# Expert rounds that serve one group of 32 slots each, with the activations turned on VectorE

## The reference

```python
logits = (x @ w_router) + b_router
top_v, top_e = lax.top_k(logits, 4)
gates = softmax(top_v)
# for each expert e, on the tokens that chose it:
gu = xe @ w_gu[e] + b_gu[e]                       # 1024 -> 2048
gate = minimum(gu[:, :1024], 7.0)
up = clip(gu[:, 1024:], -7.0, 7.0)
act = (up + 1.0) * gate * sigmoid(1.702 * gate)
y[token] += (act @ w_down[e] + b_down[e]) * gate_of(token, e)
```

## Time and profile before

| | us |
|---|---|
| median of three runs | 1610.37 |
| lowest and highest | 1606.5, 1611.21 |
| span of the profiled execution | 1606.3 |
| PE busy in it | 1577.0 (98%) |
| DVE, ACT, POOL busy | 791.2, 272.1, 209.5 |
| DMA over the span | 505.80 MB, mean 315 GB/s |

### The profile page before, as it was taken

How to read it: one execution, slowest core, us unless ns; L and a number is a source line. 1 busy time by engine, 2 the same in 40 slices (tenths; PEclk the granted TensorE clock), 3 DMA queues, 4 the chain that set the end, 5 groups by cost and what they waited for, 6 DMA issues and landing times.

```text
span 1606.3 us, 33098 instructions
## 1 busy us (share of the span) xinstructions
PE 1577.0 (98%) x13439; PEld 731.2 (46%) x13439; DVE 791.2 (49%) x1687; ACT 272.1 (17%) x554; POOL 209.5 (13%) x269
## 2 busy tenths in 40 slices
PE   9999999999999899999999999999999999999996
PEld 7677487787846333333333333333333333333332
DVE  4359639506424654445444554445444554445445
ACT  2310120006212111111111111111111111111113
POOL 3624300015100001000100001000100001000100
PEclk9999999999998899999999999999999999999998
DMA  7455746622362799999999999999999999999982
GB/s 242 153 176 191 242 165 202 234 63 112 131 257 102 262 381 404 404 402 400 404 395 405 406 404 391 405 404 403 400 393 410 402 397 395 404 404 402 400 341 106
DMA packets 72716, 505.80 MB, mean 315 GB/s; under 512 B 14577, under 2 KB 15025, under 8 KB 47434
## 3 DMA queue, kind: packets, MB, share of 16 engines
q1 hardware_dynamic: 60338, 485.32, 76.1%
q0 software_dynamic: 12320, 19.73, 4.8%
HBM read 495.93 MB, written 26.04 MB: 325 GB/s over the span
## 4 chain that ended last, share of the span: by engine, by line
PE 95%; DVE 1%; ACT 1%; issue 1%; POOL 1%; DMA 0%; SPq 0%; DVEq 0%; POOLq 0%; ACTq 0%
PE PS L1283 42%; PE PS L897 16%; PE PS L1290 14%; PE PS L1296 7%; PE PS L1206 3%; PE PS L948 2%; PE PS L1013 2%; PE PS L1327 1%; PE PS L1316 1%; PE PS L999 1%; PE PS L1063 1%; PE PS L962 1%; POOL weight_ring L604 1%; PE PS L1108 0%; PE PS L1192 0%
## 5 line engine op out<-in xcount | busy, mean ns | idle before, releaser
L1283 PE MATMUL PS<-weight_ring,region_experts 128*32 128x512 f32 x5376 | 679.4, 594 | 0.8 <-ACT region_experts L819 0.8
L1283 PEld LDWEIGHTS PS<-weight_ring,region_experts 128*32 128x32 f32 x5376 | 188.5, 110 | 345.7 <-issue 339.8
L1290 PE MATMUL PS<-weight_ring,act_turned 128*32 128x512 f32 x2048 | 231.4, 592 | 0.0
L1283 PE MATMUL PS<-ring_more,region_experts 128*32 128x512 f32 x768 | 228.2, 593 | 0.0
L897 PE MATMUL PS<-region_x,region_w 128*128 128x260 f32 (+1 forms) x928 | 209.4, 385 | 1.0 <-DVE region_x L1501 1.0
L897 PEld LDWEIGHTS PS<-region_x,region_w 128*128 128x128 f32 x928 | 175.2, 190 | 33.1 <-issue 4.6
L1681 DVE STREAM_TRANSPOSE region_experts<-region_x 32x256 f32<-32x256 f32 x384 | 166.8, 434 | 4.9
L656 POOL DMA_INDIRECT y_acc<-region_x,idx_y x31 | 49.2, 1586 | 783.0 <-ACT region_x L850 706.1
L1290 PEld LDWEIGHTS PS<-weight_ring,act_turned 128*32 128x32 f32 x2048 | 66.6, 110 | 139.5 <-issue 134.0
L1296 PE MATMUL PS<-weight_ring,act_turned 128*32 128x256 f32 x2048 | 128.9, 380 | 0.0
L1698 DVE TENSOR_TENSOR region_experts<-PS,region_w 128x512 f32<-128x512 f32 x32 | 22.1, 691 | 192.8 <-PE PS L1283 192.8
(11 more groups left out here) (290 smaller groups left out, 1288.8 us busy)
## 6 DMA issues: line engine op xcount, KB each, us to landing
weight_ring<-w_gu SPq DMA_DIRECT2D x112, 2048.0 KB, 10.3
weight_ring<-w_down SPq DMA_DIRECT2D x64, 2048.0 KB, 10.1
ring_more<-w_gu SPq DMA_DIRECT2D x16, 2048.0 KB, 13.6
region_w<-w_mt SPq DMA_DIRECT2D x33, 512.0 KB, 4.2
weight_ring<-cache_kT SPq DMA_DIRECT2D x64, 256.0 KB, 4.0
weight_ring<-cache_v SPq DMA_DIRECT2D x64, 256.0 KB, 3.9
weight_ring<-w_out SPq DMA_DIRECT2D x2, 2048.0 KB, 10.2
weight_ring<-bias_strip SPq DMA_DIRECT2D x1, 2560.0 KB, 12.2
```

Source lines behind the costliest of these rows:

```text
L1283: mm = pe.matmul(out[GRP * j:GRP * j + GRP], hTe[u][:, k, GRP * g:GRP * g + GRP], weights(c, u)[:, k, :], start=(k == 0), stop=(k == KD - 1))
L1290: pe.matmul(bank(3)[GRP * j:GRP * j + GRP], actT[:, k, GRP * g:GRP * g + GRP], w_dn[:, k, 512 * q:512 * q + 512], start=(k == 0), stop=(k ...
```

## The change

- A gate/up chunk is now two of the eight contraction blocks k, with all 2048 columns, ordered in four quarters of 256 gate and the 256 up columns that belong to them. A round serves one group g: its four matmuls side by side take the same 32 stationary columns and the four quarters of one k (`gu_step`). All four chunks are read in each round; chunk 0 has two places, and slots are freed in the third round (`gu_free`).
- With that, one partition block of a bank holds gate and up of the same columns of one group, and DVE's `group` does the whole activation of a group behind its round.
- One DVE transpose of 128x256 a group (32x32 blocks) writes `actT`. The rows of `w_down` are ordered to match. The eight PE transposes and the three ACT copies are gone.
- The gate of a slot is applied by ACT in the copies to `ysc`, six of them instead of four; `spread_gates` sums the gate parts by six small reductions, behind a new wait of DVE for `y_ready`.
- `down_wide` has groups 0 and 1, `down_rest` group 2; `down_wide` runs over all k before `down_rest`.
- 96 slots instead of 128 in `compare`, `pick`, gather and scatter; the bias has 512 columns instead of 1536.
- The down chunks lie in slots 0 and 1, gate/up in 2 to 5; so gate/up of expert 0 is loaded early and down late.

```diff
-            def ring_load(c, e):
-                if c < 4:
-                    src = w_gu[bass.ds(e, 1), c].rearrange("a p x -> (a p) x")
...
+            def gu_load(c, e, u=0):
+
+                src = w_gu[bass.ds(e, 1), c].rearrange("a p x -> (a p) x")
+                more = c == 0 and u
+                sp.dma_start(W7[:, :] if more else W6[:, slot(2 + c):slot(3 + c)], src).then_inc(r_full[6 if more else 2 + c], 16)
+
+            def down_load(c, e):
+                src = w_down[bass.ds(e, 1), c].rearrange("a p x -> (a p) x")
                 sp.dma_start(W6[:, slot(c):slot(c + 1)], src).then_inc(r_full[c], 16)
...
-            def load(b, e, u, second=True):
+            def load(b, e, u, whole=True):
                 n = b * NE + e
-                sp.wait_ge(S["round_done"], (n - 1) * ROUNDS + 1)
-                ring_load(0, e)
+                if whole:
+                    gu_load(0, e, u)
                 sp.wait_ge(S["b_wide_done"], n)
                 bias_load(e)
-                if second:
-                    second_load(e, u)
-                sp.wait_ge(S["round_done"], (n - 1) * ROUNDS + 2)
-                ring_load(2, e)
+                for c in range(1, 3):
+                    sp.wait_ge(S["gu_free"], (n - 1) * 3 + c + 1)
+                    gu_load(c, e)
                 sp.wait_ge(S["round_done"], (n - 1) * ROUNDS + 3)
-                ring_load(3, e)
+                gu_load(3, e)
                 for c in range(2):
                     sp.wait_ge(S["down_done"], (n - 1) * 2 + c + 1)
-                    ring_load(4 + c, e)
+                    down_load(c, e)
...
+                    for h in range(2):
+                        act.activation(ysc[u][0:64, 512 * h:512 * h + 512], bank(3)[64 * h:64 * h + 64], ACT.Copy,
+                                       scale=gate_a[u][64 * h:64 * h + 64])
                     act.wait_ge(S["down_done"], ne * 2 + 2)
...
+                    for j in range(4):
+                        ins = act.activation(ysc[u][64:CAP, QW * j:QW * j + QW], bank(4, QW)[GRP * j:GRP * j + GRP], ACT.Copy,
+                                             scale=gate_b[u][GRP * j:GRP * j + GRP])
+                    ins.then_inc(S["y_ready"], 1)
...
+            def gu_step(g, u, k):
+
+                for q in range(4):
+                    mm = pe.matmul(bank(g)[GRP * q:GRP * q + GRP], hTe[u][:, k, GRP * g:GRP * g + GRP],
+                                   weights(k // 2, u)[:, k % 2, SEG * q:SEG * q + SEG], start=(k == 0), stop=(k == KD - 1))
+                return mm
...
-                    pe.wait_ge(r_full[0], (ne + 1) * 16)
-                    pe.wait_ge(r_full[6 if u else 1], (b * (NE // 2) + i + 1) * 16)
                     pe.wait_ge(S["hTe_ready"], b * SELS + e + 1)
-                    gu_round(bank(0), u, ((0, 0), (0, 1), (0, 2), (1, 2)))
+                    for k in range(KD):
+                        if k == 0:
+                            pe.wait_ge(r_full[6 if u else 2], (b * (NE // 2) + i + 1) * 16)
+                        elif k % 2 == 0:
+                            pe.wait_ge(r_full[2 + k // 2], (ne + 1) * 16)
+                        mm = gu_step(0, u, k)
+                    mm.then_inc(S["round_done"], 1)
                     pick(b * SELS + e + 2, e + 1, 1 - u)
...
+                    for k in range(KD):
+                        mm = gu_step(2, u, k)
+                        if k in (1, 3, 5):
+                            mm.then_inc(S["gu_free"], 1)
+                    mm.then_inc(S["round_done"], 1)
+
+                    pe.wait_ge(S["actT_ready"], ne * ROUNDS + 2)
                     pe.wait_ge(S["y_ready"], ne + 1)
...
+                    for kk in range(KD):
+                        if kk % 4 == 0:
+                            pe.wait_ge(r_full[kk // 4], (ne + 1) * 16)
+                        mm = down_wide(kk)
+                    mm.then_inc(S["wide_done"], 1)
+                    pe.wait_ge(S["actT_ready"], ne * ROUNDS + 3)
+                    for kk in range(KD):
+                        mm = down_rest(kk)
+                        if kk % 4 == 3:
+                            mm.then_inc(S["down_done"], 1)
...
+            def group(ne, g):
+
+                gu, sg, a = gu_t[g % 2], sg_t[g % 2], act_t[g % 2]
+                n = ne * ROUNDS + g + 1
+                dve.wait_ge(S["round_done"], n)
+                dve.tensor_tensor(gu, bank(g), b_wide, ALU.add).then_inc(S["biased"], 1)
...
+                dve.transpose(actT[:, :, GRP * g:GRP * g + GRP], a.rearrange("p (k x) -> p k x", k=KD)).then_inc(S["actT_ready"], 1)
...
-                    index(b * SELS + e + 2, 1 - u, floats=last and u == 0)
...
+                    group(ne, 0)
+                    slot_rows(b * SELS + e + 2, 1 - u, taken=ne + 1, floats=last and u == 0)
+                    group(ne, 1)
+                    group(ne, 2)
```

More of the change, by code:

```diff
@@ L268, in build_step @@
         sum4 = small(201, 5)
-        gcol = [small(206 + n) for n in range(2)]
-        spare = small(208)
-        unused = [small(209 + n) for n in range(2)]
+        gate_a = [small(206 + n) for n in range(2)]
+        gate_b = [small(208 + n) for n in range(2)]
+        spare = small(210)
+        unused = [small(211 + n) for n in range(2)]
         top_v = part(WR, 3936, NTILE, 8)
@@ L493, in experts @@
                         load(b, i * 2 + u, u)
-            second_load(1, 1)
-            load(0, 1, 1, second=False)
+            gu_load(0, 1, 1)
+            load(0, 1, 1, whole=False)
             experts(0, 1)
@@ L1272, in weights @@
             def weights(c, u):
-                if c == 1 and u:
-                    return W7[:, :].rearrange("p (k x) -> p k x", k=KD)
-                return W6[:, slot(c):slot(c + 1)].rearrange("p (k x) -> p k x", k=KD)
-            w_dn = W6[:, slot(4):slot(6)].rearrange("p (k x) -> p k x", k=KD)
-            def gu_round(out, u, units, ks=range(KD)):
-                for k in ks:
-                    for j, (c, g) in enumerate(units):
-                        mm = pe.matmul(out[GRP * j:GRP * j + GRP], hTe[u][:, k, GRP * g:GRP * g + GRP], weights(c, u)[:, k, :], start=(k == 0), stop=(k == KD - 1))
-                if k == KD - 1:
-                    mm.then_inc(S["round_done"], 1)
@@ L1298, in down_rest @@
+            def down_rest(kk):
+                for j in range(4):
+                    mm = pe.matmul(bank(4, QW)[GRP * j:GRP * j + GRP], actT[:, kk, 64:CAP], w_dn[:, kk, QW * j:QW * j + QW],
+                                   start=(kk == 0), stop=(kk == KD - 1))
                 return mm
@@ L1614, in _, with spread_gates @@
             L(dve.tensor_scalar(posv[:, :, 0:NE], rt_eg[:, :, 0, :], -1.0, None, ALU.add))
+            def spread_gates(src, u):
+                for h in range(2):
+                    dve.tensor_reduce(gate_a[u][64 * h:64 * h + 64], src[0:64], AX.X, ALU.add)
+                for j in range(4):
+                    ins = dve.tensor_reduce(gate_b[u][GRP * j:GRP * j + GRP], src[64:CAP], AX.X, ALU.add)
+                ins.then_inc(S["gates_set"], 1)
             def gates():
@@ L1671, in slot_rows @@
                 dve.tensor_tensor(idx_i[u][0:CAP, :], sl[0:CAP, 0:1], unused[u][0:CAP], ALU.subtract).then_inc(S["idx_ready"], 1)
+                if taken is not None:
+                    dve.wait_ge(S["y_ready"], taken)
+                    spread_gates(sl[:, 3:6], u)
             def keep(u):
@@ L1740, in pair @@
                     dve.sem_inc(S["may"], 1)
-                    turn_rows(1 - u)
+                    if not (last and u == 1):
+                        turn_rows(1 - u)
                     if last and u == 0:
```

215 lines of the change are left out of this document (78 added, 137 removed).

## The result

The changed kernel takes 1596.1 us (median of four runs, 1593.89 to 1597.41) beside 1609.88 us for the kernel before on the same chip: a ratio of 0.9917, interval 0.9903 to 0.9932. It is faster by 13.8 us where 34.6 were forecast; the time lies in the range, near its upper end. Its profiled execution spans 1595.5 us.

What follows compares the result with a forecast made beforehand. PE was taken to pace the kernel, with DMA 1.2 us an expert behind. Savings of 28.6 us (28 experts), 5.7 (four others) and 0.3 (end) made 34.6; span 1571.7 plus 4.1 gave 1576 us, range 1563 to 1602.

Steps and rivals of the forecast that it cites:

- What bounds the kernel before: Expert stage: PE, without gaps, paces the loads at 32.72 us an expert; DMA needs 31.5, only 1.2 less.
- PE's own need: PE's work in one expert once the transposes are gone: 31.25 to 31.3 us.
- The price of the transposes on PE: Two sets of four 128x128 transposes an expert: 1.42 us x 32 experts, 45.4 us, all on the path.
- The transpose on DVE: Each new 128x256 transpose, three an expert, taken at 0.434 us, at most 1.74; hidden.
- DVE's margin of 1.8 us: Gathered rows turned on DVE at 29.5 us of an expert, wanted by PE at 31.3; 0.5 at dear transposes.
- rival (c): DVE or the gather becomes late, rows turned 1 us after PE wants them: 32.3 an expert, 1597 us; chance 0.07.
- The mechanism: Gate/up chunks, freed late and wanted early, let DMA pace the stage after two or three experts; small first-round PE waits.
- the need of DMA: Per expert, 29.3 us for six weight loads plus 2.2 for indirect gather and scatter: 31.5 us.
- the wait at chunk 3: Gate/up chunk 3 lands at 35.7, wanted at 36.4: margin 0.7 us, then 0.2 us an expert above DMA's 31.5.
- (a): DMA's lower rate late in an expert is contention, not waiting: 32.1 to 32.7 an expert, 1589 to 1608 us; chance 0.22.
- (b): PE waits 2 us at chunk 3 each first round and its clock may drop: 1629 to 1680 us; chance 0.13.
- (d): DMA has more to give, PE alone paces the experts: 45.7 us won, 1564.6 us; chance 0.10.

Runs made afterwards that it cites:

- run 1: Kernel before without its eight PE transposes an expert, ScalarE copying the activations unturned, old load schedule kept: 1572.4 us, ratio 0.9776.
- e4_noboth: Kernel after with gather and scatter bounded to row 0, so nearly no token rows move: 1562.9 us (one run).
- e12_bal128_inter: Kernel after with the kernel before's slot order, gather and scatter over 128 slots, groups 0 and 1 in one double round, earlier slot_rows: 1571.5 us.
- Runs 8, 10, 11 and 13 to 15: Kernel after, old slot order, 128 slots 1589.2 us; gather only 128 1589.5; run 1 at 96 1628.8; e12_bal128_inter with gather 96 1612.1, scatter 96 1585.7, gather 112 1615.3.
- e9_ord128: Kernel after with gather and scatter over 128 slots again, its own slot order kept: 1600.1 us.
- e8_bal128: Kernel after with the kernel before's slot order and gather and scatter over 128 slots: 1589.2 us.
- run 2: Kernel after with groups 0 and 1 served chunk by chunk in one double round, slot_rows earlier, PE awaiting the routing's count before the stage: 1594.9 us, ratio 0.9919.
- Run 3: Kernel after with gate/up chunk 3 of later experts loaded for only 64 of 128 partitions: 1642.0 us (one run).

## Why the prediction was wrong

**Right.** What bounds the kernel before (PE, with DMA 1.2 us an expert behind it): run 1 removes PE's work alone and gets 36 us. PE's own need, 31.25 to 31.3: 31.38 in e4_noboth and e12_bal128_inter. The price of the transposes on PE, 45.4 us: PE's busy time falls from 1577.0 to 1531.3 in e4_noboth, 45.7. The transpose on DVE at 0.434: it took 0.45. DVE's margin of 1.8 us: the rows are turned at 1046.27 + 5.36 = 1051.63, and the next expert begins behind the down product at about 1053.4; rival (c) did not happen. The mechanism, that the period becomes that of the loads, through a wait on gate/up in the first round: the chain shows just that, with chunk 3 as the one that ends last.

**Wrong: the need of DMA, 31.5 us an expert.** The sum was 29.3 for the weights and 2.2 for the indirect transfers, taken from the earlier trace rows of the kernel before as if the change left them alone. It did not. The diff takes both transfers from 128 slots to 96; I counted that line as fewer compare columns and a smaller pick, and put no price, not even bounds, on the gather and the scatter themselves. No term of the sum stood for that edit. What the runs showed in its place is 32.33 us an expert in the kernel after, against 31.38 without the rows (e4_noboth, 33 us less in all). Runs 8, 10, 11 and 13 to 15 show the price of 96 slots in the order of the kernel before: 15 us in the new schedule, 56 in the old one, 48 in the double round. In the order of the kernel after, 96 slots alone cost nothing against 128 (e9_ord128, 1600.1), so there the number, the order and the schedule have to change together. The rest of the DMA sum was sound: with 128 slots, the old order and the double round (e12_bal128_inter) the engines deliver 13.1 MB in 31.38 us and PE waits for chunks 1.1 us in all, and in e1_noturn an expert bound by its loads takes 31.55 to 31.90.

**Wrong: the size of the wait at chunk 3.** The forecast gave 0.7 us of margin, used up after two or three experts, and 0.2 us of stall on top of DMA's need; so its middle lay 11.4 us above PE alone (1576.0 to 1564.6). With 128 slots in the old order (e8_bal128, 1589.2) the kernel lies 26.3 us above PE alone (e4_noboth, 1562.9): 18.8 us are waits for gate/up, 0.6 an expert, and 5.4 us are a longer busy time of PE (1536.7 for 1531.3), which comes with the waits, by what isn't shown. When chunk 3 is wanted 5.2 us later, with the gather 2.6 us earlier, the waits go to 1.1 us and the busy time to 1534.5. The direction was right and the term less than half of what it is; how much of it is the due time alone stays open, since that edit changes both.

Both together make the miss of 20.1 us. It would be some 3.5 us more without luck: the forecast put the median 4.1 us above the span, and it lies 0.6 above it, so that in spans the miss is 23.8 us (1571.7 to 1595.5). As the change stands, giving back the 128 slots and their order wins only 6.9 us (1596.1 to 1589.2), because its new order had already made good 8.5 us of what the 96 slots cost (1604.6 to 1596.1); the other 13.2 us (1589.2 to 1576.0) are the second step.

**Why one run misled.** The edit of run 2 gives 1.2 us on the kernel after, costs 15.2 with 96 slots in the other order, and gives 17.7 with 128. So two causes cover each other; the reading, which is argued, is that while the transfers are slow, DMA is behind whatever is wanted when. The 24.6 us between the kernel after and e12_bal128_inter agree with the waits that went, 25.9 to 1.1. Why the double round costs time with 96 slots in the order of the kernel before isn't settled; PE waits less often there (24 times for 30) and longer (39.8 us for 33.8).

**The rivals.** (a), DMA's late stretch is contention, gave 1589 to 1608 and the result lies there, but its reason falls: in the kernel before that stretch was waiting for issues, since run 1 uses it and moves 416 GB/s. The contention is one that the change itself makes. (b) needed 2 us of wait an expert; the kernel after has 0.84, and its clock is at 1.00 in the stretches above. Run 3, with waits of up to 4.5 us, a granted clock of 0.66 behind one of them and PE busy for 15.6 us longer than in the kernel after, shows that (b)'s price was real: 1642. (d), PE alone paces, 1564.6, is what e12_bal128_inter comes near to: it has the routing's count on its path (4.1 us, first line of its waits), a price of the double round.

**What stays open.** That, in the order of the kernel before, 128 slots are good and 96 and 112 bad is shown; why, is not. The Trainium skill, DMA: Bandwidth & Descriptors, section "The descriptor swizzle", says that in a transfer over 128 partitions each of the 16 engines writes eight partitions that share one port, so that no two engines meet at a port. If an indirect transfer is dealt in the same way, then with 8 slots an engine its rows go to the port that the engine fills anyway, and with 6 or 7 they go to a neighbour's port, where both queue. The runs agree with this in what they can show (0.61 us a piece beside the rows at 128 slots, 0.74 to 0.77 at 96 and 112, and only for the gather, which writes to SBUF; the scatter, which reads from it, leaves the pieces at 0.62), but no record here names an engine or a port.

## What to carry to other kernels

When the DMA engines are full, how an indirect transfer is cut is part of its price: shortening it to the slots in use saved no bytes and made the weight loads beside it a fifth to a quarter slower. Time it at 128 slots with indices out of bounds for the rest and at the shorter length, and with more than one order of the slots: here 128 won by 15 to 56 us in one order and lost by 4 in the other. In a diff, price every line that changes a transfer's shape, even one that only makes it smaller. And when two causes can each hold an engine back, an experiment that removes one of them and shows nothing hasn't acquitted it; try it again in the kernel where the other is gone.

## What the runs showed of the hardware that was not expected

- In the runs named above, a gather over 96 or 112 slots raises the time of the 16 KB pieces of loads beside it from 0.61 us to 0.74 to 0.77; over 128 slots it leaves them at 0.61.
- Behind the issue of three chunks at once the pieces are slow without any rows: 1.3 us each in the 2.5 us from 1055.5 on in e4_noboth.
- The order of the tokens in the slots moves this kernel by 26 us at 96 slots (1596.1 to 1622.1) and by 11 at 128 (1589.2 to 1600.1), and the order that is better at 96 is the worse one at 128.
- With a load of 64 partitions under way the rate was 193 GB/s, with the engines' share at 1.01 (e3_half3, one run).
- The DMA engines of this core keep up 415 to 419 GB/s in each stretch of 100 us from 600 to 1300 us while PE is at 100.00 (e12_bal128_inter).
- DVE's transpose in 32x32 blocks takes as long for 128 partitions (0.45 us for 256 columns) as for 32 (0.434).
